# Modulation weights in wide tiles and four parts, with the first products between the parts, in a two-block transformer kernel

## What is computed

```python
mod = jax.nn.silu(c) @ w_ada[l] + b_ada[l]                  # c: 1 x 2048, w_ada: 2048 x 12288
shift1, scale1, gate1, shift2, scale2, gate2 = jnp.split(mod[:, None, :], N_MOD, axis=-1)
h = rms_norm(x, norm1_gain[l]) * (1 + scale1) + shift1      # 256 x 2048
proj = h @ w_in                                             # first 7680 columns, stage PROJ1
...
x = x + gate1 * mixing_sublayer(h, ...)                     # stages SB, DIL, GLA, BRANCH, OUT1
h = rms_norm(x, norm2_gain[l]) * (1 + scale2) + shift2
x = x + gate2 * swiglu(h, w_ffn_in[l], w_ffn_out[l])        # stage FFN
```

## Time and profile before

| | kernel before |
|---|---|
| median of 3 runs | 3319.59 us |
| profiled execution, its own time | 3319.41 us |
| its span, first to last instruction | 3317.6 us |
| PE busy | 2943.1 us (89%) |
| DVE busy | 2031.9 us (61%) |
| ACT busy | 1469.9 us (44%) |
| mean DMA rate | 204 GB/s |
| mean granted TensorE clock | 0.939 of full |

### The profile page before, as it was taken

One profiled execution on the slowest core, in us unless ns is written; L12 is line 12 of the kernel. 1 busy time (PEld: TensorE's weight loads), 2 busy tenths in 40 slices (PEclk: granted clock), 3 DMA queues, 4 the chain that ended last, 5 costly groups with the idle time before them and its releaser, 6 DMA issues.

```text
span 3317.6 us, 39306 instructions
## 1 busy us (share of the span) xinstructions
PE 2943.1 (89%) x12879; PEld 2390.8 (72%) x12879; DVE 2031.9 (61%) x2434; ACT 1469.9 (44%) x1748; POOL 13.0 (0%) x21
## 2 busy tenths in 40 slices
PE   1399994779999979999999989976869999999989
PEld 0388873458887868888888868854767887877767
DVE  6877754247777554555454554437544557989874
ACT  0144434234444344444434444424334445777763
POOL 0000000000000000000000000000000000000000
PEclk9999995679999989999999999966979999999989
DMA  8888870038888535556555656610414557999964
GB/s 299 287 287 284 280 240 15 4 103 282 287 279 289 180 120 188 190 187 196 189 192 183 197 146 191 195 34 13 130 56 175 187 183 265 367 352 359 360 250 140
DMA packets 363663, 676.83 MB, mean 204 GB/s; under 512 B 23801, under 2 KB 114321, under 8 KB 363041
## 3 DMA queue, kind: packets, MB, share of 16 engines
q1 hardware_dynamic: 362048, 669.29, 60.5%
q0 software_dynamic: 1504, 6.08, 0.6%
HBM read 673.17 MB, written 2.10 MB: 204 GB/s over the span
## 4 chain that ended last, share of the span: by engine, by line
PE 74%; DVE 5%; ACT 3%; issue 1%; DMA 0%; DVEq 0%; ACTq 0%; POOL 0%; POOLq 0%
PE bank L616 22%; PE bank L618 22%; PE bank L617 22%; PE bank L1062 1%; PE bank L882 0%; PE bank L809 0%; ACT big L1181 0%; DVE alo L1629 0%; PE bank L812 0%; PE bank L886 0%; DVE big L2082 0%; PE bank L884 0%; DVE big L2047 0%; ACT whi L1165 0%; PE bank L1074 0%
## 5 line engine op out<-in xcount | busy, mean ns | idle before, releaser
L1591 DVE TENSOR_TENSOR wlo<-raw,whi 128x1024 fp32r<-128x1024 f32 x572 | 692.7, 1224 | 525.4 <-ACT whi L1159 520.1
L616 PE MATMUL bank<-whi,ahi 128*128 128x512 f32 x2400 | 942.8, 393 | 15.4 <-DVE wlo L1591 4.3
L618 PE MATMUL bank<-whi,alo 128*128 128x512 f32 x2400 | 937.8, 391 | 0.0
L617 PE MATMUL bank<-wlo,ahi 128*128 128x512 f32 x2400 | 937.6, 391 | 0.0
L1159 ACT ACTIVATE whi<-raw 128x1024 fp32r<-128x1024 f32 x572 | 601.4, 1059 | 634.7 <-PE bank L618 578.0
L616 PEld LDWEIGHTS bank<-whi,ahi 128*128 128x128 f32 x2400 | 453.0, 189 | 110.1 <-issue 7.1
L618 PEld LDWEIGHTS bank<-whi,alo 128*128 128x128 f32 x2400 | 452.6, 189 | 95.1
L617 PEld LDWEIGHTS bank<-wlo,ahi 128*128 128x128 f32 x2400 | 453.2, 189 | 92.9
L1152 ACT ACTIVATE whi<-raw 128x1024 fp32r<-128x1024 f32 x248 | 262.6, 1061 | 501.2 <-PE bank L618 361.1
L1779 DVE TENSOR_TENSOR wlo<-raw,whi 128x1024 fp32r<-128x1024 f32 x248 | 301.9, 1224 | 182.3 <-ACT whi L1152 182.1
L616 PE MATMUL bank<-whi,bhi 128*128 128x512 f32 x944 | 370.5, 393 | 32.6 <-DVE wlo L1591 32.6
(11 more groups left out here) (426 smaller groups left out, 2163.0 us busy)
## 6 DMA issues: line engine op xcount, KB each, us to landing
raw<-in_w_in SPq DMA_DIRECT2D x296, 512.0 KB, 4.5
raw<-in_w_ada SPq DMA_DIRECT2D x192, 512.0 KB, 5.1
raw<-in_w_ffn_in SPq DMA_DIRECT2D x352, 256.0 KB, 3.0
raw<-in_w_expert_gate SPq DMA_DIRECT2D x128, 512.0 KB, 5.3
raw<-in_w_expert_up SPq DMA_DIRECT2D x128, 512.0 KB, 6.2
raw<-in_w_expert_down SPq DMA_DIRECT2D x128, 512.0 KB, 6.4
raw<-in_w_ffn_out SPq DMA_DIRECT2D x88, 512.0 KB, 4.4
raw<-in_w_out SPq DMA_DIRECT2D x64, 512.0 KB, 4.4
```

The costliest lines, as they stand in the source:

```text
L616: mm(o, shi[:, kc, T], whi[:, s, c], start=st, stop=False)
L617: mm(o, shi[:, kc, T], wlo[:, s, c], start=False, stop=False)
L618: ins = mm(o, slo[:, kc, T], whi[:, s, c], start=False, stop=en)
L1591: V.tensor_tensor(wlo[:, t % 4], raw[:, t % 8], whi[:, t % 4].bitcast(F32), ALU.subtract)\
```

## The change

The stage ADA goes. Modulation tiles now hold one 128-row chunk by 1024 columns (one DVE instruction for a tile in place of two), and the 24 groups become 12 double ones. The first four, the parts, each take 512 columns of shift1 and the 512 of scale1 that belong to the same four chunks of the norm, as two pieces of each row; the other eight are 1024 columns in a row. Part 0 (16 tiles) runs alone. Meanwhile ACT and PE finish the unmodulated norm, transposed, into `xnt`. From then on, when a part's sums are known, `lead_store` makes shift and gain of four chunks, ACT applies them (`modulate`; it writes `ahi` as well), and DVE makes `alo` (`lead_lo`). Parts 1 to 3 each have 22 tiles: 16 of modulation, and between them the six product tiles of the first three column groups that need the four chunks of the part before (`PART_ORDER`). Six more follow part 3 (`t_last`). PROJ1's loop then has three rounds of 48 tiles (32 products, 16 of modulation) for the other 12 groups. BRANCH keeps its 16 modulation tiles for each round, as one double group. OUT1 gets one double group: 48 tiles where it had 32. Squares of the first norm go to ACT's free buffers, and its scaling moves from DVE to ACT. The sum of modulation tiles stays 192.

```diff
+        ADA_PARTS, LEAD = 4, 3
+        PART_ORDER = [False] * 6 + [True, False] * 6 + [False] * 4
+
+        def lead_tile(part, i):
+
+            return 16 + 22 * (part - 1) + i
+        t_last = lead_tile(ADA_PARTS, 0)
+        t_proj1 = t_last + 6
+        t_branch = t_proj1 + 3 * 48
...
-        n_proj1, n_branch = 0, 15
+        n_proj1, n_branch = LEAD, 15
...
-            for s in range(8):
-                load(s, w_ada_v[:, 2 * s:2 * s + 2, 0:COLS])
-            with sp.Fori(1, ADA_FIRST) as g:
-                for s in range(8):
-                    load(s, w_ada_v[:, 2 * s:2 * s + 2, bass.ds(g * COLS, COLS)], g)
-
-            def ada_src(k, g):
-                return w_ada_v[:, 2 * k:2 * k + 2, bass.ds(g * COLS, COLS)]
+            def ada_part(part, k):
+                return w_ada_v[:, k, 0:2, part * COLS:(part + 1) * COLS]
+
+            def ada_src(k, w):
+                return w_ada_wide[:, k, bass.ds(w, 1)].rearrange("p w h n -> p (w h) n")
...
-            with sp.Fori(0, 7) as g:
-                for k, (is_product, j) in enumerate(PROJ1_ORDER):
-                    src = in_src(j % 8, g * (2 * COLS) + (j // 8) * COLS) if is_product else ada_src(j, g + ADA_FIRST)
-                    load(t_proj1 + k, src, g * 3)
-            for k in range(8):
-                load(t_proj1 + 7 * 24 + k, in_src(k, 14 * COLS))
...
+            def lead_src(part, i):
+                return in_src(2 * part + i % 2, (i // 2) * COLS)
+            for k in range(16):
+                load(k, ada_part(0, k))
+            for part in range(1, ADA_PARTS):
+                seen = 0
+                for i, is_product in enumerate(PART_ORDER):
+                    load(lead_tile(part, i), lead_src(part - 1, seen) if is_product else ada_part(part, i - seen))
+                    seen += is_product
+            for i in range(6):
+                load(t_last + i, lead_src(3, i))
+            with sp.Fori(0, 3) as g:
+                for k, (is_product, j) in enumerate(BRANCH_ORDER):
+                    src = in_src(j % 8, g * (4 * COLS) + (LEAD + j // 8) * COLS) if is_product else ada_src(j, g + 4)
+                    load(t_proj1 + k, src, g * 6)
...
+
+            def lead_product(t, part, i):
+                products(t, 0, [(ahi, alo, 4 * part + 2 * (i % 2)), (ahi, alo, 4 * part + 2 * (i % 2) + 1)],
+                         (2 * (i // 2), 2 * (i // 2) + 1), part == 0 and i % 2 == 0, part == 3 and i % 2 == 1,
+                         6 * part + i)
+
+            pe.wait_ge(S("norm_xn"), 2)
+            for k in range(DC):
+                if k >= 4:
+                    pe.wait_ge(S("norm_h"), k - 3)
+                for b in range(TB):
+                    ins = nc.tensor.transpose(bank[4 + k % 4][:, b * P:(b + 1) * P], xn[:, b, k * P:(k + 1) * P], ident[:])
+                ins.then_inc(S("norm_T"), 1)
+            pe.wait_ge(S("norm_h"), DC)
+            ada_columns(16, 0, acc[:, 0])
+            for part in range(1, ADA_PARTS):
+                pe.wait_ge(S("norm_lo"), 2 * part)
+                seen = 0
+                for i, is_product in enumerate(PART_ORDER):
+                    if is_product:
+                        lead_product(lead_tile(part, i), part - 1, seen)
+                        seen += 1
+                ada_columns(lead_tile(part + 1, 0), part, acc[:, part % 2])
+            pe.wait_ge(S("norm_lo"), 8)
+            for i in range(6):
+                lead_product(t_last + i, 3, i)
+
             def proj1_tile(k, g, par):
...
-            norm_stats("n1")
-            stage_end(act, "act")
-
+            norm_stats("n1", [bhi[:].rearrange("p k n -> p (k n)")[:, 0:D], blo[:].rearrange("p k n -> p (k n)")[:, 0:D]])
+            act.wait_ge(S("x_scale"), 1)
+            for b in range(TB):
+                A(xn[:, b], xres[:, b], ACT.Identity, scale=stat[:, 6 + b:7 + b]).then_inc(S("norm_xn"), 1)
+            for k in range(DC):
+                act.wait_ge(S("norm_T"), k + 1)
+                A(xnt[:, k], bank[4 + k % 4][:, 0:256], ACT.Copy).then_inc(S("norm_h"), 1)
+
+            def modulate(part):
+
+                act.wait_ge(S("norm_h"), DC)
+                act.wait_ge(S("gate_geff"), part + 1)
+                act.wait_ge(S("norm_lo"), 2 * part)
+                for k in range(4 * part, 4 * part + 4):
+                    kw = dict(scale=geff[:, k:k + 1], bias=modt[:, k:k + 1])
+                    A(htmp[:, k % 4], xnt[:, k], ACT.Identity, **kw)
+                    A(ahi[:, k], xnt[:, k], ACT.Identity, **kw).then_inc(S("norm_h"), 1)
 
             def proj_evac(proj, t0):
                 def ev(g, par):
                     act.wait_ge(tile_used, g * 8 + (t0 - T_ADA + 8 + 4))
                     A(proj[:, 0, bass.ds(g * COLS, COLS)], bank[2 * par][:], ACT.Copy).then_inc(evac_act, 1)
...
+            modulate(0)
+            for part in range(1, ADA_PARTS):
+                seen = 0
+                for i, is_product in enumerate(PART_ORDER):
+                    if is_product:
+                        split_item(lead_tile(part, i), 0, 6 * (part - 1) + seen, 0)
+                        seen += 1
+                if part == ADA_PARTS - 1:
+                    split_item(t_last, 0, 18, 0)
+                modulate(part)
...
-            def ada_rows(t, r, n, k, sums):
+            def ada_rows(t, r, k, sums):
 
                 dve.wait_ge(landed[t % 8], r * 16 + 16 * (t // 8 + 1))
-                w = raw[:, t % 8]
-                for c in range(2):
-                    col = silu_c[:, 2 * k + c:2 * k + c + 1]
-                    if k == 0 and c == 0:
-                        V.tensor_scalar(sums, w[:, 0], col, None, ALU.mult).then_inc(S("ada_step"), 1)
-                    elif c == 0:
-                        dve.wait_ge(lo_ready, r * 8 + t)
-                        V.scalar_tensor_tensor(sums, w[:, 0], col, sums, ALU.mult, ALU.add)\
-                            .then_inc(S("ada_step"), 1)
-                    else:
-                        dve.wait_ge(S("ada_step"), n * 8 + (k + 1))
-                        V.scalar_tensor_tensor(sums, w[:, 1], col, sums, ALU.mult, ALU.add).then_inc(lo_ready, 1)
-
-            def ada_store(n, src):
+                w = raw[:, t % 8].rearrange("p a n -> p (a n)")
+                col = silu_c[:, k:k + 1]
+                if k == 0:
+                    V.tensor_scalar(sums, w, col, None, ALU.mult).then_inc(lo_ready, 1)
+                else:
+                    dve.wait_ge(lo_ready, r * 8 + t)
+                    V.scalar_tensor_tensor(sums, w, col, sums, ALU.mult, ALU.add).then_inc(lo_ready, 1)
+
+            def ada_store(n, at, src=6):
...
+            def lead_store(part):
+
+                dve.wait_ge(S("ada_cols"), part + 1)
+                for h, at in enumerate((4 * part, 16 + 4 * part)):
+                    step(V.tensor_tensor(modt[:, at:at + 4], bank[6][:, 4 * h:4 * h + 4], vec[:, at:at + 4], ALU.add))
+                at = 4 * part
+                dve.sem_inc(S("mod_done"), 1)
+                V.scalar_tensor_tensor(geff[:, at:at + 4], modt[:, 16 + at:20 + at], 1.0, vec[:, V_N1 + at:V_N1 + at + 4],
+                                       ALU.add, ALU.mult).then_inc(S("gate_geff"), 1)
+
+            def lead_lo(part, pair):
+
+                k = 4 * part + 2 * pair
+                dve.wait_ge(S("norm_h"), DC + k + 2)
+                V.tensor_tensor(alo[:, k:k + 2], htmp[:, k % 4:k % 4 + 2], ahi[:, k:k + 2].bitcast(F32), ALU.subtract)\
+                    .then_inc(S("norm_lo"), 1)
+
+            for k in range(16):
+                ada_rows(k, 0, k, acc[:, 0])
+                if k == 6:
+                    dve.wait_ge(S("norm_ss"), 2)
+                    V.tensor_scalar(stat[:, 2:4], stat[:, 0:2], 1.0 / D, EPS, ALU.mult, ALU.add).then_inc(S("norm_var"), 1)
+                if k == 8:
+                    dve.wait_ge(S("norm_std"), 1)
+                    V.reciprocal(stat[:, 6:8], stat[:, 4:6]).then_inc(S("x_scale"), 1)
 
             def gain_eff(key, scale, gain):
...
+            for part in range(1, ADA_PARTS):
+                seen = 0
+                for i, is_product in enumerate(PART_ORDER):
+                    t = lead_tile(part, i)
+                    if is_product:
+                        split_item(t, 0, 6 * (part - 1) + seen, 0)
+                        seen += 1
+                    else:
+                        ada_rows(t, 0, i - seen, acc[:, part % 2])
+                    if i == 1:
+                        lead_store(part - 1)
+                    if i in (4, 5):
+                        lead_lo(part - 1, i - 4)
+            lead_store(3)
+            split_item(t_last, 0, 18, 0)
+            lead_lo(3, 0)
+            lead_lo(3, 1)
+            for i in range(1, 6):
+                split_item(t_last + i, 0, 18 + i, 0)
+            lead_evac(0)
+            for c in range(2):
+                proj1_split(2 * c, 0, 0)
+                proj1_split(2 * c + 1, 0, 0)
+                lead_evac(c + 1)
```

(36 more changed lines are left out.)

205 lines of the change are left out of this document (105 added, 100 removed).

## The result

The changed kernel takes 3257.86 us (median of 4 runs, 3257.04 to 3260.06) where the kernel before takes 3319.64 (4 runs, 3314.62 to 3321.37). The ratio is 0.9817, with an interval from 0.98 to 0.9834: 61.8 us faster. The forecast was 3265 us, a saving of 54.5, with a range from 3257 to 3284 us: the result lies inside, 0.9 us from its fast end. The profiled execution took 3257.36 us, its span 3255.6, against 3319.41 and 3317.6.

A forecast was written before the change was run, and what follows sets the result against it. DVE was taken to bound stage ADA, PE to bound PROJ1. From 3319.4 us, -49.0 - 1.0 - 6.2 + 1.4 + 0.3 = -54.5 gave 3265 us, range 3257 to 3284.

The forecast's parts named there:

- the likeliest case: Whole kernel: the change works as summed, 3265 us, 3258 to 3272 with the unknown paces; chance 0.61.
- the signs of being right: First product near 54 us, last lead sum 136 to 144, PE gapless from about 146 to 431, no OUT1 wait.
- Products taken out, and the modulation's matmuls: PROJ1: 18 product tiles of 2.72 us moved into the lead, -49.0 us; four fewer modulation matmuls, -1.0.
- PE's clock at the restart: PE's restart after the lead: first six matmuls at 1.2 GHz after a gap, +1.4 us.
- The pace of the new lead: Lead up to PE's restart: 82 tiles, parts 1 to 3 at 32.0 us each, restart at 146.3, -6.2 us.
- The wait of 2 us: End of part 0: DVE waits about 2 us in `lead_store` for the part's eight modulation matmuls, until 44.8.
- PROJ1, BRANCH and OUT1: Later stages: PROJ1 and BRANCH 0; OUT1 stays PE-bound despite 16 more tiles, one store left over, +0.3 us.
- B: Lead: loads stay at the 330 GB/s seen before, 1.59 us a tile, lead ends 9.4 later, 3274 us; chance 0.20.
- A: Parts 1 to 3: PE stays at 1.2 GHz throughout, each part's store 10 us late, 3295 us; chance 0.07.
- C: OUT1: DVE's additions and sums bunch so PE waits, up to 22.2 us, 3287 us; chance 0.04.
- D: Lead: tiles read as two pieces load far slower, kernel slower than before, 3332 us at 2.3 a tile; chance 0.03.
- E: Lead: `modulate` comes so late that products run only after the lead, 49 us stay, 3314 us; chance 0.02.

The follow-up runs named there:

- the late block: Changed kernel with part 3's six products between its last seven sums, one after its columns, first two t_last tiles split early; 3249.28 us, then 3252.11 us.

## Why the prediction was right, and where it was off

The saving at PROJ1's end was forecast as 49.0 + 1.0 + 6.2 - 1.4 = 54.8 us and is 60.3. The mechanism was right and one term was too small. The sum missed by some 7 us: 3257.86 us lies just below the 3258 to 3272 of the likeliest case, where the prediction had put a chance of only 0.03, and inside the range by 0.9. Of the signs of being right one failed: the last sum of part 3 was to end between 136 and 144 us and ended at 132.4. Point by point:

- **Products taken out, and the modulation's matmuls.** From PE's restart to PROJ1's end it was 333.3 us before, and is 425.49 - 139.99 = 285.5 now: 47.8 less. The forecast was 49.0 + 1.0 - 1.4 = 48.6. The 2.72 us for a tile holds. The first product came at 52.91 us (near 54 was forecast) and all 18 tiles before 132.
- **PE's clock at the restart.** Twelve matmuls took 5.29 us (139.99 to 145.28), where 2.72 is their time at full clock: the slow stretch cost 2.6 and not the 1.4 taken from the earlier trace rows. That is 1.2 us, more than the 0.8 that are missing; the other 0.4 aren't traced. The gap was 5.6 us here, behind the eight small matmuls, and 4.3 there.
- **The pace of the new lead.** This is the term that was mis-sized. -6.2 us was forecast and the restart moved from 152.49 to 139.99, -12.5. Part 0's end was right: the store at 44.5 us against 44.8. The wait of 2 us wasn't there; DVE waited 1.3 us just before, for ACT's `bhi`. The step from the last sum to the restart came out as forecast, 132.38 to 139.99 being 7.6 us, but by luck in one term. "Eight matmuls 1.9" was read from a row x8, and that row is four matmuls with two records each. The new step has twice as many, and took 1.95 us only since the clock was full there, PE coming to them 0.45 us behind its products; at the pace of the row it would be near 3.7, and it was 2.62 and 3.27 in the two other traces of the changed kernel, where the restart is 1.1 and 1.4 us later. What failed is "parts 1 to 3 ... 32.0" and "at 365 GB/s a tile takes 1.44 us". The parts took 29.97 in this trace, 3 x 2.0 = 6.1 us less (1.5 to 1.7 less for each in the two others), and the rate was 387 GB/s, 1.355 us, below the lower bound of 1.39 that the text gave. The earlier trace rows had 388 GB/s in one window of 2 us and the text took 365 instead, near the 352 to 367 of the page's best slices. In those PE is busy 39.4 to 40.0 of every 40 us (2820 to 3020 us in the kernel before), so they don't show what the DMA can give. DVE was off by about the same amount, 29.8 for a part and not 32.0: the 1.28 us of the wide sum was exact, but sums in series took 1.35 and not 1.39, a sum and a split 2.53 and not 2.65, because a split between two dependent sums covers their gap, and the 0.5 us for loose waits was not needed.
- **PROJ1, BRANCH and OUT1.** No gain or loss beyond this (60.3, 60.1 and 60.4 us at the ends of the three), so the 0.3 us that were added for OUT1's last store don't show. In OUT1 PE is busy 88.00 of 88 us; the run without the sums confirms that they are covered.

Of the rivals, **B** (the lead at 330 GB/s) is refuted by the run of the kernel before with half of its sums: 330 was DVE's rate. The run with two halves per sum has the time that it forecast, 3273.9 to its 3274, but there DVE sets the pace. **A** had its first step right. Each block began slow: from 52.91 us nine matmuls began 0.43 us apart. Its second step was wrong: they reached 0.227 us at 56.81, far from the block's end, and the clock over the lead was 0.74 to 0.75. The Trainium skill, "TensorE: Matmul & The Clock Gate", section "HAM oscillation — how this bites in real kernels", says that such bursts run slow again at each start; the trace agrees, but the slow start was covered here, since PE has 16 us of work in a part of 30. Where it counts is the restart, which has no cover. **C** fell with the 88.00 of 88 us in OUT1. **D** fell at once: tiles read as two pieces landed at 387 GB/s. **E** too: all 18 products ran before 132 us.

## What to carry to other kernels

When an engine bound by its own instructions holds the loads back, the GB/s and even the DMA's busy share (0.97 at 330) look like a full DMA. Nor do the waits of the loading queue tell: SP waited for DVE's sums 61.3 us in the changed kernel, with the DMA at its limit, and still 43.7 with half of the sums left out. Read the rate in the one stretch where nobody holds it back, and take it at its word; halving the engine's work in a run of its own tells it for sure. Work for an idle engine can be put into such a stretch for less than it saves: here a product tile cost the lead 0.92 us and took 2.72 away later, and 18 of them brought 28.3 us net. And place the last of it so that the engine comes out of the stretch busy: the same six products at the end of the last part, with one kept for the wait and the first tiles of the next stretch taken early, made PE restart at full clock in both traces. When a cost is read from a row, count what the row holds: here x8 was four matmuls.

## What the runs showed of the hardware beyond that

- One core sustained 387 GB/s from 20 to 120 us, within 382 to 392 in every fortieth of the stretch from 40 us on, with tiles of 512 KB in pieces of 2 KB and a share of 1.05 on the page's scale. The Trainium skill, "DMA: Bandwidth & Descriptors", section "Measured (HBM→SBUF, 128 partitions, SWDGE, issued from GpSimd)", has 341 GB/s for a transfer of 1 MB and advises at least that size for 75% of peak; transfers of half that size, issued from SP and some six in flight (7.9 us from issue to landing, one every 1.355), do better here.
- With the DMA at its limit the time from issue to landing of a tile rose from 5.1 us before (median, 44 to 130 us) to 7.9. The ring of eight still covers it, since eight tiles last 8 x 1.355 = 10.8 us: DVE waited 0.5 us for landings from 20 to 130 us.
- The eight matmuls of one column (sixteen records) take 1.84 to 1.95 us at full clock and up to 3.58 at 0.50. They lie on the path between a part's last sum and its use, so the clock costs 1.6 us there as well.
- From FFN's first product to the end of the span no kernel here differs, yet that stretch took 2112.6 us in the trace of before, 2111.0, 2110.1 and 2111.6 in those of the changed kernel, 2107.1 and 2110.4 in those of the late block and 2108.3 in that of the kernel before with half sums. A gain of under 5 us is better read at the end of the stage that it is made in.
- The granted clock that a profile gives for the start of the program can't be taken as it stands. In the stage ADA of the kernel before it reads 1.00, yet a group of four matmuls of one column (x8) takes 1.86 us there, at the pace of the sixteen records in 3.58 us at 0.50. The same group takes half of that in PROJ1, where PE never waits:

```profile
240.72 0.95 PE L708 MATMUL bank<-ones,xres 128*128 128x1 f32 x8
```
